# Differential attention: rotations issued ahead of the transposes, and the first softmax's exponentials kept in their PSUM bank

## What is computed

```python
for l in range(DEPTH):                       # DEPTH = 2
    q, k, v, u = jnp.split(rmsnorm(h, norm1_g[l]) @ w_in[l], ...)
    q = apply_rope(q, cos, sin)              # 4 heads, 2 parts of 64 columns each
    k = apply_rope(k, cos, sin)
    # diff_attention, per block of 128 queries, causal:
    s = einsum('bqhcd,bkhcd->bhcqk', q_blk, k) * 64 ** -0.5      # c = 0, 1
    p = softmax(where(mask, s, -inf), axis=-1)
    a = p[:, :, 0] - lam * p[:, :, 1]        # the difference of two softmaxes
    o = einsum('bhqk,bkhe->bqhe', a, v)
    h = h + concat(rmsnorm(o, sub_g) * (1 - lam_init), conv_out) @ w_out[l]
    h = h + (silu(gate) * up) @ w_down[l]
```

## Time and profile before

| | us |
|---|---|
| median of 3 runs | 2810.35 |
| lowest and highest | 2805.78, 2815.22 |
| the profiled execution | 2817.55 |
| its span in the trace | 2815.7 |
| attention of layer 0 | 181 to 283 |
| attention of layer 1 | 862 to 965 |

### The profile page before, as it was taken

How to read it: one execution, slowest core, us unless ns; L and a number is a source line. 1 busy time by engine, 2 the same in 40 slices (tenths; PEclk the granted TensorE clock), 3 DMA queues, 4 the chain that set the end, 5 groups by cost and what they waited for, 6 DMA issues and landing times.

```text
span 2815.7 us, 47433 instructions
## 1 busy us (share of the span) xinstructions
PE 2624.7 (93%) x18774; PEld 2345.1 (83%) x18774; DVE 1272.3 (45%) x2034; ACT 959.7 (34%) x1704; POOL 1274.3 (45%) x596
## 2 busy tenths in 40 slices
PE   5988999999998899999989899799999989899999
PEld 5976999999995799999968688688877777788887
DVE  5965532135796453213677644201466632230210
ACT  3334322223333332222355412332455543321221
POOL 3471566567565166556743320032211145564552
PEclk8987999999997799999989999899999999999999
DMA  4220122222221022232213100031111142222322
GB/s 126 74 76 1 61 90 86 94 89 75 91 76 46 16 76 89 79 101 78 86 60 116 35 2 2 30 120 56 53 46 46 46 146 90 90 90 90 99 95 75
DMA packets 175180, 203.92 MB, mean 72 GB/s; under 512 B 6459, under 2 KB 160662, under 8 KB 174758
## 3 DMA queue, kind: packets, MB, share of 16 engines
q1 hardware_dynamic: 171248, 199.37, 21.9%
q10 hardware_dynamic: 3766, 2.25, 0.3%
HBM read 193.22 MB, written 8.39 MB: 72 GB/s over the span
## 4 chain that ended last, share of the span: by engine, by line
PE 80%; DVE 7%; issue 4%; POOL 3%; ACT 3%; DVEq 2%; DMA 1%; ACTq 1%; SPq 0%; POOLq 0%
PE ps L720 17%; PE ps L721 17%; PE ps L722 17%; PE ps L1580 6%; PE ps L1460 3%; PE ps L826 2%; PE ps L965 2%; POOL wlo L2849 2%; PE ps L1442 1%; DVE conv L2315 1%; DVE gained L2204 1%; PE ps L1405 1%; DMA wraw<-in_w_proj_dn 1%; PE ps L1188 1%; PE ps L845 1%
## 5 line engine op out<-in xcount | busy, mean ns | idle before, releaser
L2849 POOL TENSOR_TENSOR wlo<-wraw,whi 128x2048 fp32r<-128x2048 f32 x182 | 842.0, 4627 | 972.6 <-ACT whi L1673 972.3
L720 PE MATMUL ps<-hn_hi,whi 128*128 128x264 f32 (+1 forms) x2752 | 890.7, 324 | 29.9 <-DVE h L2245 11.3
L721 PE MATMUL ps<-hn_lo,whi 128*128 128x264 f32 (+1 forms) x2752 | 878.1, 319 | 0.0
L722 PE MATMUL ps<-hn_hi,wlo 128*128 128x264 f32 (+1 forms) x2752 | 876.5, 318 | 0.0
L720 PEld LDWEIGHTS ps<-hn_hi,whi 128*128 128x128 f32 x2752 | 522.4, 190 | 69.2 <-issue 23.1
L722 PEld LDWEIGHTS ps<-hn_hi,wlo 128*128 128x128 f32 x2752 | 521.5, 189 | 36.1
L721 PEld LDWEIGHTS ps<-hn_lo,whi 128*128 128x128 f32 x2752 | 522.6, 190 | 32.0
L1673 ACT CAST whi<-wraw 128x2048 fp32r<-128x2048 f32 x182 | 346.4, 1903 | 531.4 <-PE ps L722 356.4
L720 PE MATMUL ps<-ff_hi,whi 128*128 128x264 f32 x704 | 200.9, 285 | 3.3 <-POOL wlo L2849 3.3
L722 PE MATMUL ps<-ff_hi,wlo 128*128 128x264 f32 x704 | 200.4, 285 | 0.0
L721 PE MATMUL ps<-ff_lo,whi 128*128 128x264 f32 x704 | 200.0, 284 | 0.0
(11 more groups left out here) (470 smaller groups left out, 4345.2 us busy)
## 6 DMA issues: line engine op xcount, KB each, us to landing
wraw<-in_w_in SPq DMA_DIRECT2D x54, 1024.0 KB, 5.3
wraw<-in_w_gate_up SPq DMA_DIRECT2D x44, 1024.0 KB, 5.1
wraw<-in_w_up SPq DMA_DIRECT2D x16, 1024.0 KB, 5.5
wraw<-in_w_down SPq DMA_DIRECT2D x16, 1024.0 KB, 5.0
wraw<-in_w_out SPq DMA_DIRECT2D x12, 1024.0 KB, 5.2
wraw<-in_w_down SPq DMA_DIRECT2D x16, 768.0 KB, 4.4
wraw<-in_w_down SPq DMA_DIRECT2D x16, 640.0 KB, 4.0
gate_dram<-gate_out SPq DMA_DIRECT2D x16, 256.0 KB, 2.0
```

Of the source, the lines that this page charges most:

```text
L720: nc.tensor.matmul(dst, whi[:, slot, c:c + P], rhs_hi, start=start, stop=False)
L721: nc.tensor.matmul(dst, whi[:, slot, c:c + P], rhs_lo, start=False, stop=False)
L722: return nc.tensor.matmul(dst, wlo[:, slot, c:c + P], rhs_hi, start=False, stop=stop)
L2849: nc.gpsimd.tensor_tensor(wlo[:, slot, :], wraw[:, slot, :], whi[:, slot, :].bitcast(F32), ALU.subtract).then_inc(w_split, 1)
```

## The change

Three edits, and one that follows from them. On PE, `rotated(u + 3)` is issued before `differences_turned(u)`. On ACT, the exponentials of the first softmax (c = 0) are written over the scores in their own PSUM bank; those of the second still go to `probs4`. On DVE, the difference reads the first softmax's exponentials from that bank. And since the bank is in use until then, `scores(u + 2)` waits for `diff_ready` of unit u and no longer for `exp_done`. The unit of the last 16 queries keeps both its exponentials in `probs4`.

```diff
                 def scores(u):
                     hd, t = units1[u]
                     if u >= 2:
-                        pe.wait_ge(exp_done, l * UNITS1 + (u - 1))
+                        pe.wait_ge(diff_ready, l * UNITS1 + (u - 1))
...
                     if u + 2 < UNITS1:
                         scores(u + 2)
-                    differences_turned(u)
                     if 1 <= u <= 4:
                         rotated(u + 3)
-                    elif u == 6:
+                    differences_turned(u)
+                    if u == 6:
                         conv_square_rows()
                     elif u >= 11:
                         out_fill(f)
...
-                            last = nc.scalar.activation(probs4[:, u % 2, c, 0:P * (t + 1)], s[:, c, :], ACT.Exp, bias=top,
+                            probs = s[:, 0, :] if c == 0 else probs4[:, u % 2, 1, 0:P * (t + 1)]
+                            last = nc.scalar.activation(probs, s[:, c, :], ACT.Exp, bias=top,
                                                         accum_out=mass[:, c, at:at + 1])
...
                     nc.vector.scalar_tensor_tensor(diff[:, slot, 0:keys], probs4[:, slot, 1, 0:keys], ratio[:, slot:slot + 1],
-                                                   probs4[:, slot, 0, 0:keys], ALU.mult, ALU.add).then_inc(diff_ready, 1)
+                                                   scores_of(u)[:, 0, :], ALU.mult, ALU.add).then_inc(diff_ready, 1)
```

## The result

The changed kernel took 2825.08 us (median of 5 runs, 2822.72 to 2828.41) against 2810.35 us before (5 runs, and not the 3 of the table ahead of the prediction; 2805.78 to 2815.22): a ratio of 1.0053, 95% interval 1.0040 to 1.0067. It is slower by 0.5%, 15 us. The forecast was 2822 us, with a chance of 0.68 for "slower".

A forecast was written before the change was run, and what follows sets the result against it. The prediction took a ring, DVE to PE to DVE or through ACT, to bound the attention blocks. Delays unit by unit summed to +7.0 us in layer 0 and +5.4 in layer 1: 2810.35 + 12 = 2822 us, range 2810 to 2834.

The forecast's parts named there:

- The likeliest case: Both attention blocks: scores waiting for the difference cost more than the change saves, +8.4 to +18 us; chance 0.60.
- unit 1, to difference 2: Behind difference 1, scores(3) stand ahead of the rotation instead of transposes: 2.08 - 0.69 = +1.4 us in each layer.
- unit 3, ratio and difference 4: Scores replace transposes, +0.6 / +0.1 us; difference 4 loses its layer 1 stall, ratio 4 meets POOL's squares, +0.5 / -0.6.
- unit 4, to difference 5: Scores of 384 keys, 0.92 to 1.65 us, replace transposes of 0.47 ahead of the rotation: +0.8 us in each layer.
- The order's 5.7 us: Units 1 to 4: transposes leave the stretch between difference and rotation, saving 2.7 us in layer 0, 3.0 in layer 1.
- The stalls' 3.5 us: Differences reading PSUM no longer stall behind POOL: saves 3.5 us, less what the ratios catch.
- The wait itself: Scores of unit u+2 wait for diff_ready of unit u instead of exp_done: whole price +21.6 us.
- Rival D: At the rotations: the reordering doesn't do what it says, rotations start later; part of the forecast, no chance of its own.
- A: Exposed scores run fast, PE holding the higher clock level in units 1 to 6: +5 us, 2815; chance 0.25.
- B: PE sinks to the lower clock level for good in both attention blocks: +18 and some 3 more, 2831; chance 0.08.
- Rival C: At the mask of unit u+2, the new wait is never the last one, gains stay whole: -10, 2800; chance 0.07.
- After attention PE gets nothing back: Behind the attention blocks PE is bound by its own products, so what follows is unchanged.

The follow-up runs named there:

- second trace of before: The kernel before, unchanged, profiled a second time: 2809.53 us (one run), span 2807.7, attention blocks 81.7 and 81.7 us.
- e2: The changed kernel with the old order, transposes ahead of the rotation; exponentials in the bank and the wait kept: 2828.76 us, 1.0065 of before.
- e4: The changed kernel with the first softmax's exponentials back in SBUF; wait on diff_ready and new order kept: 2839.01 us, 1.0090 of before.
- e3: The kernel before with one word changed, scores waiting for diff_ready instead of exp_done: 2832.45 us, 1.0071 of before.
- e1: The kernel before with the rotations ahead of the transposes at units 1 to 4, nothing else: 2800.97 us, 0.9951 of before.
- e5: The changed kernel with the rotation of units 1 to 4 moved ahead of the scores, which still wait for diff_ready: 2800.85 us, 0.9964 of before.
- e6: The kernel before with the rotation of units 1 to 4 ahead of scores and transposes, exponentials in SBUF, wait on exp_done: 2794.84 us, 0.9943 of before.

## Why the prediction was right, and where its terms were off

**The likeliest case came true, with its mechanism.** PE idled for a difference ahead of scores in the places named, and the masks of units 2, 7, 8 and 13 waited for PE. All masks together waited 28.7 us for scores, in 16 places, against 19.0 us in 7 places before: 4.9 us more a layer, where some 5 were forecast. The blocks grew by 7.4 and 6.8 us in the traces that the sum was made for, where it had 7.0 and 5.4. By the ends of the differences (us, measured in layer 0 and 1; forecast in brackets):

| step | layer 0 | layer 1 |
|---|---|---|
| unit 0, to difference 1 | +0.5 (+0.6) | -0.4 (+0.6) |
| unit 1, to difference 2 | +1.7 (+1.4) | +1.7 (+1.4) |
| unit 2, stall of difference 3 | -0.5 (-0.8) | -0.5 (-0.8) |
| unit 3, ratio and difference 4 | +1.7 (+1.1) | -0.7 (-0.5) |
| unit 4, to difference 5 | +1.5 (+0.8) | +2.2 (+0.8) |
| unit 5, to difference 6 | +2.2 (+1.8) | +2.2 (+1.8) |
| units 6 and 7, to difference 8 | +0.6 (+0.7) | +0.7 (+0.7) |
| units 8 to 10, to difference 11 | +0.8 (+0.9) | +1.0 (+0.9) |
| unit 11, to difference 12 | +0.6 (+0.5) | +0.6 (+0.5) |
| rest | -1.7 (0) | -0.1 (0) |

How closely the two sums agree is in part luck. Against the second trace of before the steps of units 1, 2, 5 and 11 stay as they are, but unit 3 is -0.7 us in both layers (there difference 4 stalls in both), unit 4 +2.5 in both, and the rest, for which the sum had nothing, +1.4 and +1.5. What lengthened the rest was not settled.

**Off in size, and why.** The order's 5.7 us: the step "the transposes leave the stretch between a difference and its rotation" took the rows' whole durations, 0.69 to 0.90 us, which overlap with what follows. e2 puts the gain under the wait at 1.8 us in the blocks (3.8 in units 1 to 4), some 0.3 us for two transposes. That is why unit 1 came out dearer than forecast, and part of why unit 4 did; there scores(6) also took 1.65 us in both layers, where the sum had the mean of both clock levels. The stalls' 3.5 us: e4 has 9.5 in the blocks. The 0.5 us that ratio 4 was to lose in the changed kernel didn't come, and the kernel that keeps SBUF inputs loses 1.0 there; the phase between DVE and POOL decided, and I had priced it at random. The wait itself was forecast at 21.6 us and measured at 20 (e3). Too much order gain and too little stall gain made up for one another, which is luck. Nor do the pieces add up as measured: 20 less 2 to 4 less 10 is 6 to 8 us, not 15. Most of the gap lies between e3 and e4, where the order, elsewhere a gain, shows as a loss of 7 us by the medians; it stays open.

**Rival D, and the claim it was folded into.** "The rotation can't start before the difference either" is right (197.26 after 195.20), and e1, e5 and e6 show that it was the more costly half of the mistake in the change: the same reordering without the wait gives 11 to 14 us, and with the rotation ahead of the scores the wait itself becomes affordable.

**Rivals A and B.** A had the clock wrong: of the exposed scores only scores(2) of layer 1 (0.92 us) and scores(13) (0.49) took the durations of the higher level, while scores(3), (4), (6), (7), (8) and (10) took 2.08, 0.80, 1.65, 2.08, 0.80 and 1.65 us in both layers, those of the lower. B had these durations right and its price too high, 21 us against 15. Scores(2) took 1.65 us in layer 0, which is 0.7 of the 0.9 us between the layers in the table's first line. The mean clock of the windows went from 0.77 and 0.75 to 0.71 and 0.74 (0.80 and 0.80 in the second trace of before).

**Rival C** failed at the point it named: the masks of units 2, 7, 8 and 13 waited for PE. For units 7 and 9 it held, as said. At unit 8 the prediction had DVE covered, yet the mask of unit 10 waited 0.53 us for scores(10) as well.

**The base.** "After attention PE gets nothing back" was wrong for these two traces: between difference 16 and the first product of line 2204 (2205 in the changed kernel) 1.6 us came back in layer 0 and 4.7 in layer 1, since before's traced execution ran that stretch at a granted clock of 0.52 and 0.53. The forecast as a difference to the median (2810.35 + 12) did not suffer, but 2830 for a traced execution was too high; it took 2825.

**The Trainium skill's fixed cost of a PSUM source** (VectorE: DVE Perf Modes, the section on the TRN2 errata) would have made 32 differences 65 ns longer each. They are not: 0.346 to 0.749 us, against 0.35 and 0.75 unhindered with SBUF sources.

## What to carry to other kernels

Keeping a result in the bank it came from saves a buffer and an engine's contention, but it lengthens the bank's life: look for who fills that bank next, and what stands behind that wait in its queue. In an in-order queue a reordering is worth only what stands ahead of the moved work: one call moved past the waiting scores was worth 25 us between two kernels with the same waits. Before a stall is priced as a gain, ask whether the next operation has the same inputs: where one long POOL operation held DVE (unit 0), the stall moved whole to the next such operation, and only with both changed was it gone; where POOL ran several in a row (unit 1), one stall of two went.

## What the runs showed of the hardware

Two products of 64 rows, on rows 0 to 63 and 64 to 127, take together what one takes: 2.08 us for the pair and 2.07 for one of 512 columns. At the higher clock level it is 1.13 for the pair and 1.12 for one. So to issue them apart costs PE the double time. ACT's exponentials into PSUM took 15 to 17 ns less each than those into SBUF beside them (mean 668 against 683 ns for 512 columns, 344 against 361 for 128, in layer 0 of the changed kernel). And POOL is held up as well: its product beside a stalled difference took 1.51 us where the others took 1.06, so that taking away a stall on DVE shifts POOL's work against DVE's: in e4 it came 0.44 us later than in the changed kernel, and still did so 6 us after difference 3.
